# Two layers and their setup written out in one block, the first weight blocks split one stage earlier

## What is computed

```python
c_act = jax.nn.silu(c)
for l in range(2):
    mod = c_act @ w_ada[l] + b_ada[l]
    shift, scale, gate = jnp.split(mod[:, None, :], 3, axis=-1)
    h = rms_norm(x, norm_g[l]) * (1.0 + scale) + shift
    proj = h @ w_in[l]
    ...
    x = x + gate * (merged @ w_out[l])
x = rms_norm(x, final_g)
...
h = rms_norm(x, attn_norm)
proj = h @ w_in_2
```

## Time and profile before

| | us |
|---|---|
| runs (three) | 2083.68, 2081.17, 2077.05 |
| median | 2081.17 |
| the profiled execution | 2083.85 |
| its span | 2081.7 |
| PE busy | 1937.3 (93%) |
| DVE, ACT, POOL busy | 1151.4, 761.5, 696.8 |

### The profile page before, as it was taken

One profiled execution on the slowest core, in us unless ns is written; L12 is line 12 of the kernel. 1 busy time (PEld: TensorE's weight loads), 2 busy tenths in 40 slices (PEclk: granted clock), 3 DMA queues, 4 the chain that ended last, 5 costly groups with the idle time before them and its releaser, 6 DMA issues. The chain is left out here.

```text
span 2081.7 us, 26689 instructions
## 1 busy us (share of the span) xinstructions
PE 1937.3 (93%) x10724; PEld 1560.5 (75%) x10724; DVE 1151.4 (55%) x1412; ACT 761.5 (37%) x1122; POOL 696.8 (33%) x391
## 2 busy tenths in 40 slices
PE   6999999999999699999999999969989898999994
PEld 5877889988888577789998888839878784555552
DVE  6358855555674527765556667360035335666664
ACT  3345110333222343511133222242246634555552
POOL 1359210434444246721133444324410011333230
PEclk7999999999999899999999999989979998999997
DMA  7222300214443222220021544224300067999983
GB/s 307 89 83 82 102 1 12 85 58 177 177 172 132 102 92 91 81 71 2 31 92 62 212 173 175 97 81 147 127 31 1 21 253 270 347 341 327 343 293 130
DMA packets 78010, 284.72 MB, mean 137 GB/s; under 512 B 27268, under 2 KB 27268, under 8 KB 60597
## 3 DMA queue, kind: packets, MB, share of 16 engines
q1 hardware_dynamic: 70852, 272.33, 36.4%
q0 software_dynamic: 6144, 8.40, 1.1%
q10 hardware_dynamic: 880, 2.17, 0.3%
HBM read 274.44 MB, written 23.63 MB: 143 GB/s over the span
## 5 line engine op out<-in xcount | busy, mean ns | idle before, releaser
L1406 POOL TENSOR_TENSOR wmem_r<-wmem,wmem_r 128x1024 fp32r<-128x1024 f32 x170 | 424.0, 2496 | 669.5 <-ACT wmem_r L954 669.5
L644 PE MATMUL banks<-h_hi_r,wmem_r 128*128 128x512 f32 x1632 | 512.7, 394 | 12.2 <-POOL wmem_r L1406 7.0
L644 PEld LDWEIGHTS banks<-h_hi_r,wmem_r 128*128 128x128 f32 x1632 | 309.1, 189 | 80.0 <-POOL wmem_r L1406 8.1
L954 ACT ACTIVATE wmem_r<-wmem 128x1024 fp32r<-128x1024 f32 x170 | 180.1, 1060 | 460.5 <-DMA wmem<-wstream 460.3
L644 PE MATMUL banks<-hT_r,wmem_r 128*128 128x512 f32 x816 | 319.9, 392 | 0.0
L644 PEld LDWEIGHTS banks<-hT_r,wmem_r 128*128 128x128 f32 x816 | 154.8, 190 | 32.2 <-issue 0.5
L1929 PE MATMUL banks<-wmem_r,gm_mem_r 128*80 128x512 f32 x496 | 178.9, 422 | 0.0
L2454 POOL TENSOR_TENSOR wmem_r<-wmem,wmem_r 128x1024 fp32r<-128x1024 f32 x32 | 77.0, 2407 | 244.2 <-ACT wmem_r L2004 244.2
L1606 POOL DMA_INDIRECT y_tok_dram<-ztp,y_idx x32 | 66.4, 2074 | 226.3 <-DVE ztp L2380 219.9
L665 PE MATMUL banks<-wmem_r,h_hi_r 128*128 128x256 f32 x768 | 141.3, 287 | 0.0
L1349 DVE SCALAR_TENSOR_TENSOR ztp<-xT,c_act,ztp 128x256 f32<-128x256 f32 x168 | 130.9, 779 | 6.0
(11 more groups left out here) (408 smaller groups left out, 3359.3 us busy)
## 6 DMA issues: line engine op xcount, KB each, us to landing
wmem<-wstream SPq DMA_DIRECT2D x206, 512.0 KB, 3.2
slots<-experts SPq DMA_DIRECT2D x80, 1024.0 KB, 7.2
xT<-ada SPq DMA_DIRECT2D x24, 1024.0 KB, 5.9
xT<-experts SPq DMA_DIRECT2D x16, 1024.0 KB, 6.7
slots<-ada SPq DMA_DIRECT2D x8, 1024.0 KB, 18.9
x_keep<-xT SPq DMA_DIRECT2D x2, 2048.0 KB, 7.6
xT<-x_keep SPq DMA_DIRECT2D x2, 2048.0 KB, 8.2
dil_rows<-dil_once SPq DMA_DIRECT2D x1, 2560.0 KB
```

Source lines behind the costliest of these rows:

```text
L644: mm = nc.tensor.matmul(o, r(lhs[:, k, :]), r(rhs[:, k, :]), start=(k == 0 and i == 0), stop=(k == KD - 1 and i == 2))
L954: inc(nc.scalar.activation(r(chunk(b)[0]), w, ACT.Copy), "w_high")
L1406: inc(g.tensor_tensor(r(lo), lo, r(hi), ALU.subtract), "w_split")
```

## The change

- The `Fori` is gone. `setup_*` and `layer_*` are functions that write the same instructions into one block: the setup, layer 0, layer 1. There is no barrier between them, and semaphores go on counting (`L * PER[name] + k`). They are cleared once, behind the second layer. Bank numbers go on as well: job j of layer L has bank (L * 263 + j) % 8.
- The weight blocks 0, 1 and 2 of a stage are split at the end of the stage that precedes: for the first layer 0 and 1 on ACT behind the setup's sines, 2 behind the eight `h_hi`; for the second layer and the attention 0 and 1 behind the sixth and seventh square, 2 behind the root. POOL splits them when ACT has; in the first layer block 2 waits until `h_ready` is complete.
- `mod` and `stage_sb` are gone. `mods_mem` has two halves, one of which is used while the other is filled, and the passes read it directly.
- In the setup each sum over k has two accumulators that take turns, and a tensor_tensor adds them.
- The loads of the setup: 321 of the 2737 columns of the constants come first (those that the setup needs), the others last; the weight blocks 0 and 1 right after x; block 2 and the first `lpar` after `ada`. The `lpar` of the second layer is loaded in the merge of the first. The store `x_keep` follows x_loaded or x_done and no block.

```diff
+EARLY_CONST = CCOL["ident"][0]
...
-        mods = sb("mods", [P, 32])
-        mod = sb("mod", [P, 24])
-        stage_sb = sb("stage_sb", [P, 32])
+        mods_mem = sb("mods_mem", [P, 2, 32])
...
-        acc_first = [flat_ztp[:, i * 256:(i + 1) * 256] for i in range(len(BY_DVE))]
+        acc_first = [[flat_ztp[:, (2 * i + j) * 256:(2 * i + j + 1) * 256] for j in range(2)] for i in range(len(BY_DVE))]
+        FIRST_STEPS = KD + 1
...
+            sp.dma_start(cst[:, 0:EARLY_CONST], consts[:, 0:EARLY_CONST]).then_inc(SEM["const_loaded"], 16)
+            sp.dma_start(posi[:, :], pos_in).then_inc(SEM["pos_loaded"], 16)
+            sp.dma_start(xT[:, :, :].rearrange("p k t -> p (k t)"), x_in).then_inc(SEM["x_loaded"], 16)
+            load_first(0)
+            load_first(1)
+            sp.dma_start(dist_sb, distances).then_inc(SEM["dist_loaded"], 16)
+            for b in range(1, SETUP_B):
+                load_ada(b)
+            load_first(2)
+            inc(sp.dma_start(lpar[:, :], lparams[0]), "params_loaded", 16)
+            sp.dma_start(cst[:, EARLY_CONST:NCONST], consts[:, EARLY_CONST:NCONST]).then_inc(SEM["const_rest"], 16)
...
+                at = FIRST_STEPS * i
+                for k in range(KD):
+                    w_k, c_k, acc = ada_first[:, b, k * 256:(k + 1) * 256], c_act[:, k:k + 1], acc_first[i][k % 2]
+                    if k < 2:
+                        ins = v.tensor_scalar(acc, w_k, c_k, None, ALU.mult)
+                    else:
+                        dve.wait_ge(SEM["first_step"], at + k - 1)
+                        ins = v.scalar_tensor_tensor(acc, w_k, c_k, acc, ALU.mult, ALU.add)
+                    ins.then_inc(SEM["first_step"], 1)
+                dve.wait_ge(SEM["first_step"], at + KD)
+                v.tensor_tensor(acc_first[i][0], acc_first[i][0], acc_first[i][1], ALU.add).then_inc(SEM["first_step"], 1)
...
-        with nc.Fori(0, LAYERS) as L:
-          with nc.Block() as block:
...
-            inc(nc.scalar.activation(mod[:, :], mods[:, 8:32], ACT.Copy), "mod_ready")
-            stages = glob("stage").rearrange("p (l m) -> p l m", l=LAYERS)
-            inc(nc.scalar.activation(stage_sb[:, :], stages[:, bass.ds(L, 1), :].rearrange("p a m -> p (a m)"), ACT.Copy), "mod_ready")
...
+            def high(b, l=L):
+
+                if b >= LAYER_B:
+                    b, l = b - LAYER_B, L + 1
+                if l == LAYERS:
+                    w = landed(act, b, 16 * LAYERS * LAYER_B // RING)
+                    nc.scalar.activation(r(chunk(b)[0]), w, ACT.Copy).then_inc(SEM["a_high"], 1)
+                elif b not in WHOLE:
+                    w = landed(act, b, l * PER[f"wload{b % RING}"])
+                    inc(nc.scalar.activation(r(chunk(b)[0]), w, ACT.Copy), "w_high")
...
+            if L == 0:
+                high(0)
+                high(1)
             for k in range(KD):
                 after("h_scaled", k + 1)
...
+            if L == 0:
+                high(2)
...
+                if k < KD - 1:
+                    high(FIRST["wo"] + k + RING)
             inc(nc.scalar.activation(rstd[:, :], bank("ss"), ACT.Sqrt, bias=con("eps")), "rms_sqrt")
+            high(LAYER_B + RING - 1)
...
+            low(0, 2)
+            if L == 0:
+                after("h_ready", KD)
+            low(2, FIRST["pg"])
...
+        with nc.Block() as block:
...
+            @block.vector
+            def _(dve):
+                setup_vector(dve)
+                for L in range(LAYERS):
+                    layer_vector(dve, L)
```

1837 lines of the change are left out of this document (928 added, 909 removed).

## The result

| | us |
|---|---|
| kernel before, median of 7 runs | 2077.05 (2072.05 to 2088.53) |
| changed kernel, median of 7 runs | 2063.91 (2059.83 to 2069.00) |
| ratio, 95% interval | 0.993 (0.9905 to 0.9956) |
| profiled execution of the changed kernel, its span | 2065.6, 2063.8 |

The change makes the kernel 13 us faster by the medians (9 to 20 by the interval). The predicted 2065.7 us lies 1.8 us above the measured median. The profiled executions differ by more than the medians do: that of the kernel before (2083.85 us) lies 6.8 us above the median of these runs, that of the changed kernel 1.7. So of the 17.9 us between their spans some 5 are scatter from one execution to the next.

The account below looks back on a forecast made before the run. TensorE, busy 93% of the span, was taken as the bound, with only its idle and slow stretches winnable. Gains of 4.3 + 9.8 + 1.4 = 15.5 us off the 2081.17 us median gave 2065.7 us, range 2056 to 2073.

Parts of the forecast that it names:

- (a): Setup loads: 184 KB less ahead of the ada block DVE waits for, so DVE starts its sums 0.45 us sooner.
- (b): Setup sums: two accumulators cut the pitch from 0.52 to 0.40 us, giving 1.5 us over five blocks.
- (c): Setup: POOL's two moved splits fall on DVE's last two blocks of sums and cost 2.1 us each, 4.2 us.
- rival 1: Setup: the splits miss DVE's sums and fall on the reciprocal; 4.2 us more won, 2061.5 us, chance 0.15.
- (d): First layer's pass, now free of POOL: after first product and its rounding PE starts at 45.8 us.
- (e): PE's 48 matmuls at the first layer's start, 12 of them slow, take 13.3 us; PE reaches r2 at 59.1.
- Between the layers: Passage from first to second layer: no branch, barrier, table load or copies, splits in the tail; 9.8 us won.
- Rival 3: Between the layers: the gap was not the loop's, so 5 us of it stay; 2070.7 us, chance 0.05.
- Into the attention: Passage from second layer to attention: pass free of POOL's splits, PE's fp32 sums end sooner; 1.4 us won.
- Rival 2: First layers' r3: weight blocks come too late for the faster start; 2.5 us lost, 2068.2 us, chance 0.15.
- Rival 4: Whole layers: straight code is fetched too slowly and stalls PE; 45 us cost, 2095 us, chance 0.04.
- I count nothing: Within the layers: little register work before loads and PE hardly waits for splits, so no gain or loss.

Follow-up runs that it names:

- dma_order: Changed kernel with the setup's loads in their old order (constants whole and early, weight blocks and lpar behind ada): 2065.72 us, ratio to before 0.9941.
- blocks: Changed kernel with setup, first layer and second layer each in its own block, so barriers but no loop: 2073.22 us, ratio to before 0.9986.
- copies: Changed kernel with mod and stage_sb copied again on ACT at each layer's head: 2064.17 us, ratio to before 0.9913.
- warm: Kernel with POOL's splits gated away from DVE's work, plus 21 unused matrix products filling PE's stops between stages: 2054.31 us, ratio to before 0.9863.
- home: Changed kernel with splits of blocks 0 to 2 back at the heads of second layer and attention: 2069.86 us, ratio to before 0.9963.
- Before_late2: Kernel before with two unused 128x512 additions behind mods in the setup, delaying the first layer: 2081.66 us, ratio to before 1.0017.
- gated: Changed kernel with ACT's first splits behind the setup's root and POOL's waiting on DVE's steps, in setup and tails: 2062.62 us, ratio to before 0.9932.
- twin: Changed kernel run once more, nothing edited: 2064.48 us.

## Why the prediction was right, point by point

- **(a) Bytes, DVE 0.45 us sooner.** Right in size, as far as it can be told: the two first traces say the opposite (17.89 us after 17.63), but the means of ten and four traces differ by 0.38 us in the forecast's sense. It is less than the start varies by itself (0.7 us among the ten), and in the profiled execution PE and not DVE ends the setup, so it was worth nothing there.
- **(b) The sums, pitch 0.40.** Right: six in 2.46 us, 0.41 apart. The added tensor_tensor was priced too high, so a block took 3.36 us and not 3.6, and the five 20.7 us where they took 22.8. Little of these 2.1 us reached `mods`, whose first instruction starts at 41.17 us where it started at 41.61, because PE then ends the setup. That PE's own products at 1.2 GHz (6.99 us for 32), which DVE had hidden before, would bound this stage was in no step.
- **(c) The splits, 4.2 us.** The price was right (4.1 in dma_order), the place wrong. POOL began at 38.57 us and not at 35, since ACT waited 2.74 us for the store of `dil_once`; the splits missed the sums, as rival 1 had it, but into the gap before `mods` and not onto the reciprocal. They cost 1.7 us, all of it on L561, so the term was 2.5 us too large. With no split beside it (blocks, copies, dma_order, warm) the same instruction takes 0.17. The Trainium skill, "SBUF — State Buffer", section "Who interferes with whom", draws the line between two SBUF inputs and one; the traces agree down to an instruction of eight elements a partition (L561, 1.86 us for 0.17) beside one that reads PSUM (L559, 0.17).
- **(d), (e) PE's start.** The pass to PE 1.66 us, PE to r2 12.96, forecast 1.5 and 13.3. The first layer's head gave 5.55 us, forecast 4.3.
- **Between the layers**, 9.46 us against 9.8. The pass 0.11 us behind `rstd`, PE to r2 13.17 (13.3). The tail grew by 0.67 us, not 0.4: the last but one sum of squares was held, as forecast, but took 1.49 us and not 1.2 (the last took 0.69). The split of the gain was told wrongly: "5.0 the start of the pass, 4.2 POOL's splits" reads as two edits, but home and blocks show that most of both needs the barrier gone: home, without barrier and loop and with the splits where they were, has 8.5 of the 9.46 us. Rival 3 fell: the gap is 0.40 us with a barrier and without a loop.
- **Into the attention**, 2.98 us against 1.4: 1.9 up to the end of PE's sums, 1.0 behind them, where the next 16 products took 5.18 us and not 6.21.
- **Rival 2** did not come: PE passes from r2 on without a wait for a split, and in the whole layer only pg2 waits, 3.7 us. **Rival 4** neither: 88 packets, and a single "issue" wait of PE in the first layer, 1.0 us, as in the kernel before. Its 2095 us does not follow from its terms: 45 us on top of 2065.7 are 2111.
- **"I count nothing" for the layers.** This is the step that failed. Its reason was that PE hardly waits for splits within a layer, and that stayed so; what it left out is that PE's clock falls behind other stops when the layer starts at another time. 8.9 us came back, by the estimate above 6.3 of them in stretches at half clock, behind stops of 0.8 to 3.8 us that both kernels have. The remaining 2.6 us are not in the time at 0.50. Before_late2 shows one way to lose up to 2.0 us so, by the order of stretch and stop; whether that is all of it is open. The prediction's own sign shows the miss: PE was to be at r2 again 652 us after the first time, and came 658.5 us after it (661.8 before).
- **The rest**, 8.8 us shorter, was counted as unchanged. In the fourteen traces it takes 671 to 686 us, over products that are all the same but for warm's few. Most of that spread is the clock again: behind the attention's head PE works for 52.9 us at 0.50 in the trace of the kernel before, for 39.1 in the changed kernel's and for 25.5 in gated's, which is that kernel's fastest run and has the shortest rest. At half the time lost, 6.9 of the 8.8 us are that. Whether the change has a part in it is open: the trace of the kernel before is one of its slower executions, and home's rest takes 684 us. Without it the heads' 18.0 less the layers' 8.9 would have been 9 us; the medians say 13.

## What to carry to other kernels

A barrier between stages costs its own 0.4 us (0.9 ahead of the attention), and whatever the engines could have done ahead of it: here POOL's splits, which fell from a free reciprocal onto a pass that they slowed by 2.1 us each. When work that slows its neighbour is moved, its price is known well and its place badly; a wait on the neighbour's real end (as in gated's tails) fixes the place. And when the head of a stage is moved, the stage behind it is not the same stage at another time: PE's clock falls at other stops, which took back 8.9 us in these traces, nearly as much as the largest single gain (9.46). Such a loss, and the start of an engine by a few tenths of a microsecond, vary from one execution to the next, and one pair of traces does not settle them.

## What the runs showed of the hardware

- PE at a granted clock of 0.50 loses half of the stretch while busy, and within the layers every such stretch follows a stop of 0.8 to 3.9 us within otherwise full work. Which stops are followed by one was the same in two executions of the changed kernel (twin), differed in one place of the second layer between two of the kernel before, and differed between the changed kernel and home, whose first layers have the same work up to the tail and start within 0.05 us. The Trainium skill, "TensorE: Matmul & The Clock Gate", section "What's actually happening", says that the slow start of one kernel varies from run to run with the phase at the kernel's start, and that the ramp costs less than 1% of a typical kernel. The traces agree in size: the difference between two orders of the same work was 4.9 us in one layer of 630 (0.8%), and that between the changed kernel and home 3.7 us.
- What a slow stretch costs depends on what comes next: ahead of a wait for another engine up to 2.0 us were got back (a stop of 1.06 us for 3.10), behind it nothing.
- Keeping PE busy with unused products held the clock at 1.00 over the stop of 6 us between the layers, and cost nothing where PE had to wait.
- A reciprocal of 128x512 takes 3.34 to 3.35 us with a POOL split inside it, in the changed kernel, gated and home alike.
